# Woven high and low weights, with other address remainders for the activations, in a macaron SSD and pooling block

## What is computed

```
x = x + 0.5 * swiglu(rms_norm(x, g1), w_gate1, w_up1, w_down1)      # 1024 -> 2816 -> 1024
h = rms_norm(x, g_mix);  proj = h @ w_in                            # 1024 -> z 1024, xBC 1536, dt 16, u 1024
y_ssd  = chunked state-space scan of silu(conv(xBC)), dt; times silu(z); grouped rms_norm
y_pool = per 256 channels: (trailing mean over 2/4/8/16 frames - u) @ pool_w, scaled
x = x + concat([y_ssd, y_pool]) @ w_out                             # 2048 -> 1024
x = x + 0.5 * swiglu(rms_norm(x, g2), w_gate2, w_up2, w_down2)
return rms_norm(x, final_norm)
```

## Time and profile before

| | us |
|---|---|
| median of 2 runs (1039.58 to 1040.51) | 1040.05 |
| profiled execution | 1040.21 |
| its span, first to last instruction | 1038.4 |
| PE busy in it | 1028.7 |
| PEld busy | 847.2 |
| DVE busy | 559.5 |
| ACT busy | 380.3 |
| POOL busy | 178.8 |

### The profile page before, as it was taken

How to read it: one execution, slowest core, us unless ns; L and a number is a source line. 1 busy time by engine, 2 the same in 40 slices (tenths; PEclk the granted TensorE clock), 3 DMA queues, 4 the chain that set the end, 5 groups by cost and what they waited for, 6 DMA issues and landing times.

```text
span 1038.4 us, 13577 instructions
## 1 busy us (share of the span) xinstructions
PE 1028.7 (99%) x4798; PEld 847.2 (82%) x4798; DVE 559.5 (54%) x686; ACT 380.3 (37%) x489; POOL 178.8 (17%) x166
## 2 busy tenths in 40 slices
PE   9999999999999999999999999999999999999997
PEld 7888888888888878878787888888888888888887
DVE  5544444444344468786799795554444444433442
ACT  6433223323333337652324753432233223333322
POOL 1110111101001132221063452110101101101100
PEclk9999999999999999999999999999999999999999
DMA  6533323322333343222222233333333322233222
GB/s 185 150 113 101 100 86 96 101 83 67 100 99 96 102 128 96 82 81 75 68 81 81 62 102 102 101 102 95 88 100 101 99 87 87 79 110 96 88 65 81
DMA packets 188873, 99.09 MB, mean 95 GB/s; under 512 B 3780, under 2 KB 188200, under 8 KB 188840
## 3 DMA queue, kind: packets, MB, share of 16 engines
q1 hardware_dynamic: 188168, 97.60, 32.4%
q10 hardware_dynamic: 672, 1.05, 0.3%
HBM read 96.54 MB, written 2.10 MB: 95 GB/s over the span
## 4 chain that ended last, share of the span: by engine, by line
PE 95%; DVE 3%; issue 1%; ACT 1%; POOL 0%; ACTq 0%; POOLq 0%
PE bank L1152 29%; PE bank L1154 29%; PE bank L1153 29%; PE bank L1224 1%; PE bank L1218 1%; PE bank L1221 1%; PE bank L1473 1%; PE bank L1475 1%; PE bank L1474 1%; PE bank L1286 0%; PE bank L1308 0%; PE bank L1276 0%; DVE w_lo_part L745 0%; DVE ebuf L905 0%; PE bank L1192 0%
## 5 line engine op out<-in xcount | busy, mean ns | idle before, releaser
L1152 PE MATMUL bank<-xghi,w_hi_part 128*128 128x512 f32 x960 | 377.3, 393 | 0.0
L1154 PE MATMUL bank<-xghi,w_lo_part 128*128 128x512 f32 x960 | 373.7, 389 | 0.0
L1153 PE MATMUL bank<-xglo,w_hi_part 128*128 128x512 f32 x960 | 373.6, 389 | 0.0
L745 DVE TENSOR_TENSOR w_lo_part<-w_raw,w_hi_part 128x1024 fp32r<-128x1024 f32 x194 | 253.9, 1309 | 191.3 <-ACT w_hi_part L500 185.9
L500 ACT ACTIVATE w_hi_part<-w_raw 128x1024 fp32r<-128x1024 f32 x194 | 203.9, 1051 | 194.5 <-PE bank L1154 193.0
L1152 PEld LDWEIGHTS bank<-xghi,w_hi_part 128*128 128x128 f32 x960 | 180.2, 188 | 39.7 <-issue 2.8
L1153 PEld LDWEIGHTS bank<-xglo,w_hi_part 128*128 128x128 f32 x960 | 180.3, 188 | 38.2 <-issue 1.2
L1154 PEld LDWEIGHTS bank<-xghi,w_lo_part 128*128 128x128 f32 x960 | 180.2, 188 | 38.0
L412 POOL TENSOR_TENSOR gate_buf<-gate_buf,rstd 128x512 f32<-128x512 f32 x44 | 56.9, 1294 | 424.4 <-ACT gate_buf L523 424.4
L1152 PE MATMUL bank<-acthi,w_hi_part 128*128 128x512 f32 x330 | 129.0, 391 | 0.0
L1154 PE MATMUL bank<-acthi,w_lo_part 128*128 128x512 f32 x330 | 128.5, 389 | 0.0
(11 more groups left out here) (223 smaller groups left out, 804.2 us busy)
## 6 DMA issues: line engine op xcount, KB each, us to landing
w_raw<-in_ffn_w_gate SPq DMA_DIRECT2D x42, 512.0 KB, 3.8
w_raw<-in_ffn_w_up SPq DMA_DIRECT2D x42, 512.0 KB, 3.8
w_raw<-in_w_in SPq DMA_DIRECT2D x29, 512.0 KB, 3.8
w_raw<-in_ffn_w_down SPq DMA_DIRECT2D x32, 384.0 KB, 3.2
w_raw<-in_ffn_w_down SPq DMA_DIRECT2D x32, 320.0 KB, 3.0
w_raw<-in_w_out SPq DMA_DIRECT2D x16, 512.0 KB, 3.6
out<-xtok SPq DMA_DIRECT2D x4, 512.0 KB, 3.4
xload<-in_x SPq DMA_DIRECT2D x3, 512.0 KB, 7.1
```

The lines of the kernel that those rows point to most:

```text
L745: dve.tensor_tensor(wlo[:, slot(m)], raw[:, slot(m)], whi[:, slot(m)].bitcast(F32), ALU.subtract).then_inc(w_lo, 1)
L1152: pe.matmul(bank, w, h, start=first and n == 0, stop=False)
L1153: pe.matmul(bank, w, l, start=False, stop=False)
L1154: mm = pe.matmul(bank, wl, h, start=False, stop=last and n == blocks - 1)
```

## The change

The high and low parts of the weights are no longer two tensors. One tensor of the same total size holds them woven: for each weight the high part and 4 bytes behind it the low part. `whi` and `wlo` become views of it with a step of two elements, so that 128 weights of one kind and block span 1024 bytes. Every instruction that writes or reads the parts keeps its place, its count and its number of elements, and has a step of 8 bytes where it had 4: ScalarE's write of the high part, VectorE's read of it and write of the low part, and TensorE's weight loads. `w_raw` and the DMAs into it are unchanged.

`start_at` puts an unused filler of 64 bytes ahead of xghi, so that xghi and xglo start at addresses with remainder 192 modulo 256 (66752 and 83136), and the tensors behind them too. The shared region starts at remainder 0 (110080, before 110208). The woven weights start at 17536, remainder 128 as before.

```diff
         raw = sb("w_raw", [P, RING, UB, P])
-        whi = sb("w_hi_part", [P, RING, UB, P], F32R)
-        wlo = sb("w_lo_part", [P, RING, UB, P], F32R)
+        woven = sb("w_parts", [P, RING, UB, P, 2], F32R)
+        whi, wlo = woven[:, :, :, :, 0], woven[:, :, :, :, 1]
         xT = sb("xT", [P, DK * S])
+        def start_at(residue):
+
+            lane = (residue - nc.sbuf_base) % LANES
+            if lane:
+                sb(f"lane{nc.sbuf_base}", [P, lane // 4])
+
+        start_at(WEIGHT_LANE + 64)
         xghi = sb("xghi", [P, DK * S], F32R)
         xglo = sb("xglo", [P, DK * S], F32R)
...
-        base = nc.sbuf_base + (WEIGHT_LANE - nc.sbuf_base) % LANES
+        base = nc.sbuf_base + (WEIGHT_LANE + 128 - nc.sbuf_base) % LANES
```

## The result

| | us |
|---|---|
| before, median | 1040.05 |
| after, median of 2 runs (1063.38 to 1063.49) | 1063.43 |
| ratio after / before, 95% interval | 1.0225 [1.0181, 1.0269] |

The forecast was 1013 us, so the sign was wrong. The slowdown is clear of noise; whether it is above 2% is not, since the interval begins at 1.8%. The time lies in the range of 987 to 1082 only because the range took in rival C, the slower one.

A forecast was written before the change was run, and what follows sets the result against it. TensorE's matmul pitch was taken to bound the kernel: half of the 13.3 ns leftover on 4290 matmuls, 28.5 us, less 0.9 us given back, leaves 27.6; 1040.2 - 27.6 = 1012.6, forecast 1013 us, range 987 to 1082.

The forecast's parts named there:

- rival C: TensorE's matmul stream: streams in step meet instead of passing, slower by 19 to 57 us, middle 1078 us; chance 0.22.
- I hold somewhat likelier than not: TensorE's matmul stream: the address reading, that weight and activation streams hinder each other by their phase.
- rival B: Whole kernel: nothing measurable changes, the 13.3 ns being a fixed cost of changing weights; 1040 us; chance 0.35.
- The two distances: Activations 64 bytes ahead of weights in norm-fed units, 128 in down projections and second half of w_out; both perfect would be luck.
- the 1.8 of which the sum counted half: 460 to 565 us: 1.8 us of the gain falls where other engines share the chain; 0.9 us taken off.
- The conversions: ScalarE and VectorE, 194 conversions each with a step of 8 bytes: nothing taken as cost.
- rival D: VectorE, 460 to 600 us: conversions above 2.3 us fill it, +25 us, 1065 us; chance 0.05.
- Rival C's point of decision: TensorE: the slower case decides from 4.8 ns more per matmul, a pitch of 231.4 ns.
- the leftover: Each matmul on TensorE: about 13.3 ns above one column per cycle, 57 us in all; half expected won, 28.5 us.
- The 231 ns after a break: TensorE after four transposes at 924.29 us: steps of 231 ns against 227 settled, read as streams hindering each other.
- the dt unit with its 32 columns: Eight dt-unit matmuls with 32-column weights aren't shorter, 398 ns against 391 to 393; counted against the address reading.
- Weight loads: TensorE's weight loads: should stay at 188 ns; the pitch follows once a load exceeds it.

The follow-up runs named there:

- e2: Kernel before with contiguous weights, only the activations moved 64 bytes (norm-fed) and 128 bytes (others) ahead of the weights' remainder: 1052.57 us, ratio 1.0119.
- m4: Bare matmul stream, contiguous weights; both arrays moved together by 32 to 192 bytes: 226.7 ns each; weights alone moved by 64, 128, 192: 233.4, 232.4, 228.8 ns.
- e3: Against before, only ScalarE's and VectorE's conversions strided by 8 bytes, TensorE reading the same bytes as dense blocks (products mixed up): 1043.95 us, ratio 1.0030.
- m5: Bare matmul stream: woven weights at 64 distances, best 230.0 ns; loads reading one address 128 times 231.7 ns; contiguous at distance 240, 233.3 and 226.7 ns.
- m2: Bare matmul stream with other steps and widths: loads of 32 columns 231.6 ns at distance 0; 256-column matmuls 120.0 ns at distance 0, 113.3 at 192.
- e1: The changed kernel with the weave kept and both activation distances put back to 0: 1065.69 us, ratio 1.0247 against before.
- e4: Kernel before with contiguous weights, only xghi and xglo moved 20 bytes further on: 1076.55 us, ratio 1.0347.
- e5: The woven kernel with norm outputs and shared region both 192 bytes ahead of the weights: 1054.26 us, ratio 1.0134 against before.
- m3: Bare matmul stream, contiguous weights, activations moved through all distances 0, 4, ... 252 bytes: 226.7 ns only at distance 0, up to 240.0 elsewhere.

## Why the prediction was wrong, point by point

**Right.** TensorE's pitch bounds the kernel and was the one thing that decided. The instructions, the clock and the count stayed, and 4158 full-width matmuls times the change of pitch give the result within 1.9 us. The pitch does hang on the two address streams, which "I hold somewhat likelier than not": against rival B. The rule of the Trainium skill that the loads take nothing from the running matmul, by independent ports ("TensorE: Matmul & The Clock Gate", Part 2), is not borne out: in e2 nothing but the distance changed, and the pitch rose from 226.7 to 228.9 and 232.6, while both arrays moved together left 226.7 (m4). The two distances came out unequal, and the mixer gave back 1.7 us, about the 1.8 of which the sum counted half. The conversions cost nothing that shows in the change, as the sum had it, and rival D is out by e3. VectorE's 1291 ns with the step, 1309 without, fits the note on cachelines in the Trainium skill ("SBUF — State Buffer"), that two hits per 16-byte line keep full bandwidth; ScalarE's 1051 to 1133 does not quite, an 8% that its idle time hid. Rival C's point of decision, 231.4 ns, fits: the mean over both kinds, (2976 x 233.3 + 1182 x 231.4) / 4158 = 232.8, is just above it, and the time just above 1061.

**The step that failed** is the sign of the leftover: "About 13.3 ns per matmul are left over", read as the price of two streams that meet, which a better layout could lower. Measured, a stream whose weight load doesn't walk at all settles at 231.7 ns. The contiguous layout at distance 0 is 5 ns *better* than that, and no layout of some 320 was better. It was not a layout that a change of address could improve but the best one found. "Bounds of the gain per matmul, if the streams stop meeting: nothing at one end, the whole 13.3 ns at the other" therefore had the wrong ends: the lower one had to lie well below nothing, for the change lost 6.6 and 4.7 ns where the sum counted 6.65 as won. How much of the 13.3 ns is fixed stays open: no run streamed matmuls without a load beside each.

**What I misread.** The 231 ns after a break was put down to a stream that is hindered until it settles, and then used as a sign that settling can be improved. It is rather near the 231.7 of m5, a stream whose loads don't walk. And "against it", the dt unit with its 32 columns not being faster, was the better hint; at distance 0 smaller loads are slower (m2). As I read them now, both rows spoke for a loss when a good phase is disturbed; that reading is argued and not shown.

**Rival C** had the direction, and its price began at 231, where the result lies; its middle of 1078 was 15 us too high. Its picture, streams in step that always meet, is not shown: woven and with aligned activations, the pitch ranges from 230.0 to 234.3 over the distances, so it isn't the step alone either.

**Weight loads** were to stay at 188 ns. They rose to 193 in e1 and 195 in after. But in e4, with contiguous weights, the loads beside the norm-fed matmuls took 193 too, and those beside the others 188, so the stride isn't the only thing that lengthens a load. The load's length doesn't follow the pitch either: in e2 it stayed at 188. No load reached the pitch.

## What to carry to other kernels

A constant remainder above one column per cycle need not be a reserve: before a layout is changed to win it, run the bare stream of the same matmuls at some distances and steps; here it told the pitch of before, after, e1, e2 and e4 within 0.2 ns. For e5 it had two values, 230.0 and 233.4, and the kernel stood between them, at 230.7. For such a stream, float32 in fp32r parts with a weight load per matmul, contiguous weights with the activations on a 16-byte boundary and at the weights' remainder modulo 256 were the best found, and came back to 226.7 every time that they were run. Start from it, and measure the pitch from start to start over many matmuls. Activations moved by 20 bytes cost 3.5%.

## What the runs showed of the hardware

- Settled pitches at 512 columns gather at 226.7, 233.3 and 240.0 ns, 6.67 ns apart, which is 16 cycles at 2.4 GHz each; at 256 columns at 113.3 and 120.0. Values between are means over steps that vary, such as 229, 229, 229, 233 for 230.0 in m5, and so is the 233.3 of the norm-fed units in after, of steps of 230, 232 and 236.
- The pitch depends on the distance of the two operands (contiguous: 226.7 at 0, 228.8 at 64, 232.4 at 128, 233.4 at 192), on the step of the weights (233.3 at distance 0 with 8 bytes), and on where the moving operand starts: 4 bytes past a 16-byte boundary it took 237.8 on average in m3, 12 bytes past one 230.0, on one 232.6. Some layouts have more than one settled value (contiguous at 240: 226.7, 233.3, 236.6; woven at 192: 230.0, 233.4). Whether what ran ahead sets it or chance, no run tells apart.
- At distance 0, fewer weights to load, or one address read over and over, make the stream slower than 128 contiguous ones: 231.6 and 231.7 against 226.7 ns.
- ScalarE writes 1024 elements with a step of 8 bytes in 1133 ns and contiguously in 1051; VectorE shows no such price (1291 and 1309).

What inside SBUF makes these phases stays open: no run here looks below the pitch.
